# Token parts and output weights of the second half at a row pitch of 4096 bytes, and the last output projection started one step earlier

## The reference, cut to what matters

```python
h = rms_norm(x, norm_w[0]); z = h @ w_in0            # 1024 -> 5120
out = concat(retention branch, S5 branch) @ w_out0   # 2048 -> 1024
x = x + out
h = rms_norm(x, norm_w[1]); z = h @ w_in1            # 1024 -> 4096
q, f, i, g = split(z, 4)
o = gated linear recurrence over 8 heads (q, f, i)   # chunks of tokens
x = x + (head_rms_norm(o) * silu(g)) @ w_out1        # 1024 -> 1024
y = rms_norm(x, final_norm_w)
```

## Time and profile before

| | |
|---|---|
| median of 3 runs | 3256.62 us (3247.53 to 3258.72) |
| the profiled execution | 3251.87 us, span 3250.0 us |
| mean granted clock of PE | 0.958 of full speed |
| PE busy | 3084.8 us, 95% of the span |
| strips of `project_hgrn`, first to last | 1942.5 to 2926.0 us |
| output tiles, first to last matmul | 2961.5 to 3242.2 us |

### The profile page before, as it was taken

One profiled execution on the slowest core, in us unless ns is written; L12 is line 12 of the kernel. 1 busy time (PEld: TensorE's weight loads), 2 busy tenths in 40 slices (PEclk: granted clock), 3 DMA queues, 4 the chain that ended last, 5 costly groups with the idle time before them and its releaser, 6 DMA issues. The chain is left out here.

```text
span 3250.0 us, 45886 instructions
## 1 busy us (share of the span) xinstructions
PE 3084.8 (95%) x16972; PEld 2699.8 (83%) x16972; DVE 1502.3 (46%) x2880; ACT 1046.1 (32%) x1751; POOL 1083.0 (33%) x672
## 2 busy tenths in 40 slices
PE   7999899799999879899999979999999999997999
PEld 6999899688888669786788859999978888886886
DVE  7999254404540088876422212133345444436442
ACT  4111122312221055543211110034544433446741
POOL 2222222132222256562121202244434433445541
PEclk9999999899999989999999999999999989998899
DMA  5433655455553265555533322343343333333433
GB/s 137 105 119 121 197 173 165 116 119 154 175 155 94 86 233 202 196 196 209 186 111 115 117 107 79 92 156 101 114 145 114 116 111 104 127 111 127 137 123 109
DMA packets 376188, 442.86 MB, mean 136 GB/s; under 512 B 46264, under 2 KB 315192, under 8 KB 366832
## 3 DMA queue, kind: packets, MB, share of 16 engines
q1 hardware_dynamic: 277648, 373.05, 36.0%
q10 hardware_dynamic: 98400, 67.91, 6.8%
HBM read 285.26 MB, written 159.81 MB: 137 GB/s over the span
## 5 line engine op out<-in xcount | busy, mean ns | idle before, releaser
L796 PE MATMUL p_psum<-p_h_hi,p_w_hi 128*128 128x344 f32 (+1 forms) x1600 | 568.4, 355 | 0.0
L796 PE MATMUL p_psum<-p_h_hi,p_w_lo 128*128 128x344 f32 (+1 forms) x1600 | 562.3, 351 | 0.0
L796 PE MATMUL p_psum<-p_h_lo,p_w_hi 128*128 128x344 f32 (+1 forms) x1600 | 561.2, 351 | 0.0
L2564 PE MATMUL p_psum<-p_h_hi,p_w_hi 128*128 128x344 f32 (+1 forms) x1280 | 463.9, 362 | 8.4 <-DVE p_h_lo L2301 3.4
L2564 PE MATMUL p_psum<-p_h_lo,p_w_hi 128*128 128x344 f32 (+1 forms) x1280 | 457.3, 357 | 0.0
L2564 PE MATMUL p_psum<-p_h_hi,p_w_lo 128*128 128x344 f32 (+1 forms) x1280 | 456.7, 357 | 0.0
L380 POOL CAST p_w_hi<-p_w_raw 128x1024 fp32r<-128x1024 f32 x80 | 91.1, 1139 | 814.5 <-PE p_psum L796 672.1
L796 PEld LDWEIGHTS p_psum<-p_h_hi,p_w_hi 128*128 128x128 f32 x1600 | 302.9, 189 | 36.6 <-issue 9.3
L796 PEld LDWEIGHTS p_psum<-p_h_hi,p_w_lo 128*128 128x128 f32 x1600 | 303.0, 189 | 29.1
L796 PEld LDWEIGHTS p_psum<-p_h_lo,p_w_hi 128*128 128x128 f32 x1600 | 303.0, 189 | 28.4
L2319 DVE COPY p_out<-p_psum 128x344 f32<-128x344 f32 (+1 forms) x160 | 93.5, 586 | 484.5 <-PE p_psum L2564 484.4
(11 more groups left out here) (346 smaller groups left out, 6008.6 us busy)
## 6 DMA issues: line engine op xcount, KB each, us to landing
p_w_raw<-in_w_in SPq DMA_DIRECT2D x144, 512.0 KB, 5.0
z<-p_out ACTq DMA_DIRECT2D x64, 512.0 KB, 3.5
z<-p_out SPq DMA_DIRECT2D x64, 512.0 KB, 3.2
p_raw<-z SPq DMA_DIRECT2D x32, 1024.0 KB, 5.5
rg_raw<-z SPq DMA_DIRECT2D x16, 1536.0 KB, 7.9
c_m_raw<-m SPq DMA_DIRECT2D x16, 1024.0 KB, 7.1
u_s<-p_out SPq DMA_DIRECT2D x128, 73.0 KB, 2.8
p_shared<-u_s SPq DMA_DIRECT2D x32, 292.0 KB, 5.3
```

What stands on the lines that cost most here:

```text
L796: ins = pe.matmul(bank, wv[par][:, k, :], h[:, k, c0:c0 + n], start=(k == 0 and j == 0), stop=(k == KD - 1 and j == 2))
L2564: ins = pe.matmul(bank, wv[par][:, k, :], h[:, k, c0:c0 + n], start=(k == 0 and j == 0), stop=(k == KD - 1 and j == 2))
```

## The change

Four parts. First, `by_half` gives two views of each token buffer: the first half's as before, and one for the second half of [128, 8, 1024], which starts 64 elements (256 bytes) behind the buffer's start and has rows of 4096 bytes. All that reads or writes the second half's parts, in the three programs, and the output weights in the same space (`top_hi`, `top_lo`, `wo_hi`, `wo_lo`) take the second view. Second, `OUT` is 23: the first output tile stands in step 23, and there is one step less. Third, in step 22 PE makes the first column blocks of both last strips, then the pieces of the recurrence, then the second column blocks of both (`last_strips`); DVE evicts in that order (`evict_last`). Fourth, the output weights are loaded and split by column halves: 4 transfers of 256 rows x 512 columns for the first half, split while the second column blocks are multiplied, and 4 for the second half behind the last strip.

```diff
+SHIFT = KD * (COLS[0] - COLS[1])
+def by_half(buf):
+
+    second = buf[:].rearrange("p k c -> p (k c)")[:, SHIFT:].rearrange("p (k c) -> p k c", c=COLS[1])
+    return buf[:], second
...
-        h_hi, h_lo = sb("h_hi", [P, KD, COLS[0]], F32R), sb("h_lo", [P, KD, COLS[0]], F32R)
+        h_hi, h_lo = (by_half(sb(n, [P, KD, COLS[0]], F32R)) for n in ("h_hi", "h_lo"))
...
-                            ins = pe.matmul(bank, wv[par][:, k, :], h[:, k, c0:c0 + n],
+                            ins = pe.matmul(bank, wv[par][:, k, :], h[hf][:, k, c0:c0 + n],
...
-            return top[:, k, 0:D] if k < KD else low[:, k - KD, :]
+            return top[:, k, :] if k < KD else low[:, k - KD, :]
...
-        wo_hi, wo_lo = h_hi[:, :, 0:D], h_lo[:, :, 0:D]
+        wo_hi, wo_lo = h_hi[1], h_lo[1]
...
-        OWN, OWN_END, OUT = 10, 20, 24
+        OWN, OWN_END, OUT = 10, 20, 23
...
-            def load_weights(r):
-                if r >= 6:
-                    sp.wait_ge(wo_lo_done, r - 3)
-                sp.dma_start(wo_raw[r], a["w_out1"][r * P:(r + 1) * P, :]).then_inc(wo_ld[wo_slot(r)], 16)
+            def load_weights(half, e):
+                if half:
+                    sp.wait_ge(wo_lo_done, 2 * e + 2)
+                sp.dma_start(wo_raw[e], a["w_out1"][2 * e * P:(2 * e + 2) * P, columns(half)]
+                             .rearrange("(r p) c -> p r c", p=P)).then_inc(wo_ld[e], 16)
...
                 if k == LAST_STRIP - 1:
+                    pool.wait_ge(blk_done, blocks_to(LAST) + 2)
+                    weights(0, range(KD))
+                    pool.wait_ge(blk_done, blocks_to(LAST) + 3)
+                    split_mixed(0)
                     pool.wait_ge(blk_done, blocks_to(N_STRIPS))
-                    weights(range(4))
+                    weights(1, range(4))
...
+            def last_strips(b):
+                pe.wait_ge(w_lo_done, N_STRIPS)
+                c0, n = HBLOCKS[1][b]
+                for g in (LAST, LAST + 1):
...
             def out_part(c, half):
                 par, n = c % 2, out_no(c)[1]
+                if c == 0:
+                    pe.wait_ge(wo_lo_done, KD * (half + 1))
                 if half == 0:
-                    pe.wait_ge(wo_lo_done, KD)
                     pe.wait_ge(m_lo_done, c + 1)
```

More of the change, by code:

```diff
@@ L1931, in out_tile, with columns @@
             return k - OUT if 0 <= k - OUT < N_OUT else None
-        def wo_slot(r):
-            return r if r < 6 else r - 4
+        LAST = N_STRIPS - 2
+        def columns(half):
+            return slice(half * BLK, (half + 1) * BLK)
         def out_no(c):
@@ L2151, in split_mixed, with weights @@
                                    ALU.subtract).then_inc(m_lo_done, 1)
-            def weights(rows):
+            def weights(half, rows):
                 for r in rows:
-                    pool.wait_ge(wo_ld[wo_slot(r)], 16)
-                    pool.tensor_copy(wo_hi[:, r, :], wo_raw[r]).then_inc(wo_hi_done, 1)
+                    pool.wait_ge(wo_ld[r // 2], 16 * (half + 1))
+                    pool.tensor_copy(wo_hi[:, r, columns(half)], wo_raw[r // 2][:, r % 2, :]).then_inc(wo_hi_done, 1)
             split(0)
@@ L2275, in _ @@
                     prelude(1)
+                if k == LAST_STRIP:
+                    act.wait_ge(blk_done, blocks_to(N_STRIPS))
+                    for r in range(4, KD):
+                        act.wait_ge(wo_ld[r // 2], 32)
+                        act.activation(wo_hi[:, r, columns(1)], wo_raw[r // 2][:, r % 2, :], ACT.Copy)\
+                            .then_inc(wo_top_done, 1)
                 if 0 <= k - 1 < N_HG:
@@ L2287, in _ @@
                     turned_keys(k - 1)
-                if k == LAST_STRIP:
-                    for r in range(4, KD):
-                        act.wait_ge(wo_ld[wo_slot(r)], 16 * (1 + (r >= 6)))
-                        act.activation(wo_hi[:, r, :], wo_raw[r], ACT.Copy).then_inc(wo_top_done, 1)
                 if k + 1 < N_HG:
@@ L2563, in strip @@
                         for j, (wv, h) in enumerate(((w_hi, h_hi), (w_hi, h_lo), (w_lo, h_hi))):
[L2564 removed]
+                            ins = pe.matmul(bank, wv[par][:, k, :], h[hf][:, k, c0:c0 + n],
+                                            start=(k == 0 and j == 0), stop=(k == KD - 1 and j == 2))
+                    ins.then_inc(blk_done, 1)
+            def last_strips(b):
+                pe.wait_ge(w_lo_done, N_STRIPS)
+                c0, n = HBLOCKS[1][b]
+                for g in (LAST, LAST + 1):
+                    if b:
+                        pe.wait_ge(dmix_done, 1)
+                    else:
+                        pe.wait_ge(ev_done, blocks_to(LAST - 1) + g - LAST + 1)
+                    for k in range(KD):
+                        for j, (wv, h) in enumerate(((w_hi, h_hi), (w_hi, h_lo), (w_lo, h_hi))):
+                            ins = pe.matmul(ps[:, 2 * b + g - LAST, 0:n], wv[g % 2][:, k, :], h[1][:, k, c0:c0 + n],
                                             start=(k == 0 and j == 0), stop=(k == KD - 1 and j == 2))
```

109 lines of the change are left out of this document (64 added, 45 removed).

## The result

The changed kernel takes 3229.94 us (median of 4 runs, 3224.71 to 3230.2). The kernel before, run beside it, takes 3255.59 (4 runs, 3247.53 to 3258.72). The ratio is 0.9923, 95% interval 0.991 to 0.9935: faster by 0.8%, some 25 us. The forecast was 3209 us, a gain of 42.7; the time lies 21 us above it. It is inside the range of 3191 to 3233 but above 3224, where the forecast's own range ended: it is inside because the range was reached out to the rivals. The profiled execution took 3224.71 us for a span of 3222.8, 27.2 less than the span before.

A forecast was written before the change was run, and what follows sets the result against it. PE's own pace sets the time, except a gap before the first output block and output steps carrying the recurrence. Gains 28.7 + 6 + 8 = 42.7 us off 3251.87 give 3209 us; range 3191 to 3233, the forecast's own 3192 to 3224.

The forecast's parts named there:

- Term 1: 512-column matmuls given the new pitch: 226.7 ns each instead of 232.5, a gain of 28.7 us, bounds 0 and 31.
- L796's stretch: First program's strips: 1920 matmuls gaining 5.8 ns each, 11.1 us.
- L1779's: First output projection: only rows 0 to 7 move; a block of 48 loses 159 ns, 30 blocks give 4.8 us.
- Term 3: Own-head steps: most of eight come from clock 0.91 to 0.95; -8 us, bounds 0 and -20.
- Both rivals that denied the pace: 512-column blocks: pitch not the cause, 232.5 ns stays, 3238 us, chance 0.07; or 4096-byte rows run slower, 0.03.
- The rival of a pace that only fades: Blocks of 24: first nine matmuls at 231.1 ns, then 226.7; gain about 18 us, time 3224 us, chance 0.10.
- L1648's 2.2 us: Stretch before the first output projection: 384 matmuls, taken at the same pace, gain 5.8 ns each, 2.2 us.
- L1718's 1.1: Few matmuls, partly on rows already of the good pitch: a gain of 1.1 us at most.
- Term 2: Output tiles behind the strips: one tile less gives -11.2, a later loop end +5; -6 us, range -12 to +2.
- The loop: Steps behind tile 0, paced by `raw` loads: starts near 2970, six turns of 22.7 us, ends 3106, 5 us later.
- step 23 gives nothing back: Step 23: ACT's and POOL's queues, blocked behind loads, push the recurrence another 10 us; 3219 us, chance 0.08.
- sign of being wrong: Prediction is wrong if blocks of 24 still take 5.58 us, or own-head steps stay at 37.4 us.

The follow-up runs named there:

- Experiment 1: Kernel before with only the new row layout in all three programs; step order, last strips and weight loads unchanged: 3228.6 us, ratio 0.9934.
- experiment 4: Kernel before with a stretch of isolated matmuls in front, varying row start, pitch or width: 226.5 ns from start 0, 233.5 from 32 bytes at 4096 pitch.
- experiment 5: Changed kernel with its second view begun 224 instead of 256 bytes behind the buffer's start, rows still 4096 bytes apart: 3254.7 us, ratio 1.001.
- experiment 6: Kernel before with another stretch of isolated matmuls in front, more starts and widths: 226.9 ns from 256 bytes, 233.1 from 128, 233.3 from 192.
- Experiment 2: Changed kernel with the old row pitch of 4128 bytes, keeping the earlier output tile, strip order and weights by column halves: 3252.55 us, ratio 0.9999.
- Experiment 7: Kernel of experiment 3 with DVE's last four subtractions of the second column half moved ahead of score mask, `p_mixed` and `p_q_ref`: 3220.34 us, ratio 0.9899.
- experiment 3: Changed kernel with the four loads of the second weight column half issued one step earlier, ahead of `raw`: 3222.1 us, ratio 0.9909.

## Why the prediction was right, and where it was wrong

**Term 1, the pitch: the pace right, its cause put one step off.** Forecast -28.7. L796's stretch gave 11.2 for 11.1 and L1779's 4.7 for 4.8. Experiment 1 has the whole measured gain with the rows alone, 0.66% or some 21 us; terms 1 and 3 together had 36.7 for it. Both rivals that denied the pace fell: at the higher clock a block of 24 takes 5.44 us (10.88 for 48), not 5.58, and rows exactly 4096 bytes apart did no harm. The rival of a pace that only fades was right in that it fades, but a group of 48 behind shifted rows loses only 0.8 ns a matmul (L151 against L143 in experiment 4), 40 ns in all. The step that needs mending is the reading of the earlier trace rows, "a cost of rows that are shifted by 32 bytes from one to the next". At 512 columns it is where a row begins that costs, not how far it lies from the one before it (experiments 4 and 5). With the pitch of 4128 only row 0 of each eight began at a multiple of 256 bytes. The change's offset of 256 bytes thus matters as much as its pitch of 4096: with 224 the gain is gone. The Trainium skill ("TensorE: Matmul & The Clock Gate", section Back-to-back issue gap) has no such part in its distance of two matmuls. Experiments 4 and 6 contradict it: 229 to 233 ns against 227, at 512 columns and one pitch, by the start alone.

Two entries of the term were wrong. L1648's 2.2 us did not come: PE's work in that stretch fell from 414.87 to 412.81 us (both from windows of the stretch), but the stretch took 464.02 instead of 464.08. Its idle time there rose from 49.2 to 51.2 us, so a faster PE only waited longer. One of these waits is for DVE's low parts, 15.4 us in 11 waits before and 16.2 us in 13 now (the changed kernel's: us, times, longest); where the rest went was not followed:

```profile
PEld rg_psum L1656 <- DVE rg_h_lo L1430: 16.2, 13, 3.2
```

L1718's 1.1 lay in the same stretch and did not come either. And 0.9 us were lost in the first half of the second program, where nothing was changed; at a clock of 0.97 in both, I have no cause for it.

**Term 2, the earlier start: failed.** Forecast -6. Measured: the stretch to the last `raw` is 11.95 us longer, one tile less gives back 11.2, and the tail is 1.6 shorter than the sum of its parts, so -0.9. Experiment 2 agrees: its ratio of 0.9999 (0.9988 to 1.001) leaves room for 4 us, not for 6. The loop was as forecast, even a little better: six turns of 22.35 us for the 22.7 I took, 2.1 us to the good. What failed was the time at which the loop starts, 53.2 us behind the last strip (2954.45 - 2901.23) instead of 44. The 9.2 us, by the prediction's own stations:
- "So they leave from 2931", 5 us behind the strips: it was 7.4. I had left out that the queue waits at the load of `raw` for the stores, and these wait for two evictions behind eight subtractions.
- "landing at 2940", 9 us behind the issue: 10.7 us.
- From landing to DVE's first subtraction, 7 us forecast, 5.1 measured: 1.9 us to the good.
- "Eight subtractions (5.8 us) and three recurrence operations" to 2955, 8 us: 12.35 us (2924.47 to 2936.82).
- Block (0, 1) in 6 us: 8.56.
- From its end to the loop's first load 9.1 us for the 9 forecast.

Of these, the biggest is the subtractions. The first four of the second column half (`p_xt`), and all eight that read `p_xn`, four of each half, by their line (least, median, longest in ns, first and last start):

```profile
L2503 DVE TENSOR_TENSOR p_h_lo<-p_xt,p_h_hi x4: 681/685/1762, 2924.5 to 2926.3; 128x512 fp32r<-128x512 f32 x4
...
L2503 DVE TENSOR_TENSOR p_h_lo<-p_xn,p_h_hi x8: 1092/1520/1751, 2897.5 to 2935.2; 128x512 fp32r<-128x512 f32 x8
```

The shortest are at 0.68, the 0.7 that I took from the earlier trace rows. The last of the first four took 1.76, and the four behind the score mask 6.25 together, 1.56 each. POOL began its own work on the decay and the keys (L2124) at 2925.70 and was busy to the end. The Trainium skill ("SBUF — State Buffer", section Who interferes with whom) says that a DVE instruction with two SBUF inputs contends with a GpSimd instruction that reads SBUF. The durations agree. In the same stretch the score mask, which has one input in PSUM, took 0.68 us beside POOL, and the product for `p_q_ref`, with both in SBUF, 1.38:

```profile
2927.96 0.68 DVE L2403 TENSOR_TENSOR p_score<-p_psum,p_causal 128x512 f32<-128x512 f32 x1
...
2929.16 1.38 DVE L2416 TENSOR_TENSOR p_q_ref<-p_q_ref,p_raw 128x512 f32<-128x512 f32 x1
```

Experiment 7 takes 1.1 us off the second group (5.16 for 6.25) without freeing it, since POOL's key work still runs beside it; a kernel without that overlap was not tried. That the late loads and the spread subtractions made the delay is shown by experiments 3 and 7: block (0, 1) starts 5.7 and 10.0 us earlier, with strips that end within 0.6 us of the changed kernel's, and the spans are 4.6 and 8.7 us shorter.

The rival "step 23 gives nothing back" had come closest: its price was 10 us, and 7 were measured here. Its sign, "a gap over 20 us", was there in two parts, 10.7 and 11.0 us with 1.1 us of work between them, and its mechanism is the one in the chain: ACT's queue behind the loads pushes the recurrence. The prediction had looked for one gap of 10 to 18 us.

**Term 3, the clock: the direction right, the size wrong, what decides it open.** Forecast -8, "if most of the eight steps come to 0.95". The stretch of the second half gave 9.5 us in all, of which term 1 claims 7.8, so 1.7 for the clock. Windows of the changed kernel, an own-head step at each of the levels (they answer to the last two of the earlier trace rows):

```profile
2503.40:2537.23 33.83, 33.83 (x201) 28.92 (x200) 17.61 (x31) 15.49 (x30) 14.37 (x12) 1.00 0.32 102
...
2648.28:2685.31 37.03, 37.03 (x201) 31.21 (x200) 17.69 (x31) 15.49 (x30) 14.37 (x12) 0.91 0.38 121
2685.31:2720.75 35.44, 35.44 (x202) 30.03 (x200) 17.61 (x31) 15.48 (x30) 14.37 (x12) 0.95 0.38 127
```

A step that comes to 0.95 gives 1.6 us, as forecast (1.5). But only one more of them did, and the first own-head step, which was 35.90 at 0.95 before, went to 33.83 at 1.00. The steps that stayed at 0.91 gave 0.4 us each for the 0.56 of term 1. I had taken two thirds of the possible gain with no row that said how many steps would change. Kernels with the same code up to there have one or two short steps, and not the same ones (experiments 3 and 7, the changed kernel), so neither number nor place can be had from the code. The term should have been one or two steps, -2, with the same ends.

**The sum.** Neither sign of being wrong came: blocks of 24 went to 5.44 us, and own-head steps from 37.4 to 37.0. Of the 15.7 us by which the profiled execution misses the forecast, 6.3 lie in the second half's strips (term 3), 7.1 in the stretch behind them (term 2), 3.2 in the stretch of L1648 and L1718 and 0.9 in the first half of the second program; the tail gives 1.6 back. The stretches that came out as forecast differ by rounding. The other 5 us of the 21 are the profiled execution's place below the median of its kernel. Before the change it also lay below the median, by 3.7 us, and the forecast was added to that execution and not to the median. The forecast gain was 42.7 us and the measured one 25: the time is inside the range, but only term 1's pace was forecast well.

## What to carry to other kernels

Where PE paces a kernel with fp32r matmuls of 512 columns, look at where each row of the moving operand begins, not only at how many columns it has: starts at multiples of 256 bytes from the buffer's start gave 2.5% of the time of these matmuls here for no work. A step that is moved one place ahead gains only what its slowest input lets it: follow that input's queue back past the stores and evictions ahead of it, and price elementwise work on DVE by rows in which POOL runs beside it. A clock that falls in every step of a loop gives gains in lumps (1.6 us a step here), and which steps get them differed here even between kernels with the same code in them; time such a kernel more than once, and do not put more than a lump or two into a forecast.

## What the runs showed of the hardware that was not expected

- fp32r matmuls of 512 columns follow one another at 226.5 to 227.7 ns when the moving row starts 0 or 256 bytes behind the buffer's start, 229.2 at 64, 231.7 to 233.5 at 16, 32, 128 and 192. From 320 to 512 columns (146.7 to 226.9 ns, experiment 6) a column costs 1 / 2.4 ns; at that rate 512 columns are 213.3 ns, so some 13 ns are paid even at the best start.
- 344 columns took 157.7 ns from a start of 0 in experiment 6, right behind 48 of 336 columns, but 153.3 in experiment 4 (L187, the same start, behind 512-column ones). With a start of 32 bytes it was 156.9. This is open.
- At 256 columns the order turned round: 119.8 ns from 0, 117.9 from 32 bytes (experiment 4, L199 and L203). At 504 the start of 32 bytes cost nothing (226.7 ns, L207). Only at 512 columns did every comparison show the loss.
- Eight more matmuls in a step made it 35.65 us, shorter than the 37.0 without them, when the clock stayed at its higher level through it.
